# A three-part network on one core: modulation columns taken in pairs, h and k made between the weight blocks, one weight tile in four multiplied as float32

## The reference

```python
silu_c = jax.nn.silu(c)
silu_cc = jax.nn.silu(c_ctx)
shift, scale, gate = jnp.split(silu_c @ w_ada[l] + b_ada[l], 3, axis=-1)
shift_c, scale_c, gate_c = jnp.split(silu_cc @ w_ada[l] + b_ada[l], 3, axis=-1)
h = _modulate(_rmsnorm(xs, norm_g[l]), shift[:, None], scale[:, None])
hc = _modulate(_rmsnorm(cs, norm_g[l]), shift_c, scale_c)
pc_kv = hc @ w_l[:, OFF_K:OFF_ZA]
p = h @ w_l
```

## Time and profile before

| | before |
|---|---|
| median of 3 runs | 2229.89 us (2226.3 to 2232.34) |
| the profiled execution | 2231.75 us, its span 2230.1 us |
| PE busy | 2096.8 us, 94% of the span |
| DVE, ACT busy | 1357.2 us (61%), 1120.2 us (50%) |
| weight tiles split on ACT and DVE | 338, two units each |
| granted TensorE clock, mean | 0.973 of full |

### The profile page before, as it was taken

How to read it: one execution, slowest core, us unless ns; L and a number is a source line. 1 busy time by engine, 2 the same in 40 slices (tenths; PEclk the granted TensorE clock), 3 DMA queues, 4 the chain that set the end, 5 groups by cost and what they waited for, 6 DMA issues and landing times.

```text
span 2230.1 us, 32794 instructions
## 1 busy us (share of the span) xinstructions
PE 2096.8 (94%) x13142; PEld 1879.5 (84%) x13142; DVE 1357.2 (61%) x1766; ACT 1120.2 (50%) x1502; POOL 49.2 (2%) x60
## 2 busy tenths in 40 slices
PE   4879999999999997999999999999899999999996
PEld 3668888879999887899998788888689999998785
DVE  4864665556665555466676566766754643776554
ACT  5842445544443345244446666666544443775433
POOL 0000000000000000000000000010000000000000
PEclk9989999999999998999999899999999999999998
DMA  9942542347885554345555455555544455434552
GB/s 352 338 170 95 170 168 98 117 131 275 272 281 170 189 189 142 123 161 188 171 189 176 146 188 187 188 171 206 176 140 153 149 184 162 123 116 165 194 189 76
DMA packets 204236, 394.66 MB, mean 177 GB/s; under 512 B 6726, under 2 KB 25916, under 8 KB 201692
## 3 DMA queue, kind: packets, MB, share of 16 engines
q1 hardware_dynamic: 199584, 369.78, 49.7%
q0 software_dynamic: 2880, 17.40, 2.0%
q10 hardware_dynamic: 1660, 5.90, 0.7%
HBM read 390.89 MB, written 2.16 MB: 176 GB/s over the span
## 4 chain that ended last, share of the span: by engine, by line
PE 85%; DVE 6%; ACT 4%; issue 2%; DMA 2%; ACTq 0%; DVEq 0%; POOL 0%; SPq 0%
PE ps L1841 13%; PE ps L1843 13%; PE ps L1842 13%; PE ps L1829 12%; PE ps L1831 12%; PE ps L1830 12%; ACT w_hi L449 2%; DVE w_lo L1037 2%; DMA tables<-in_tables 1%; PE ps L2023 1%; PE ps L2001 1%; DVE tables L1352 1%; PE ps L2192 1%; PE ps L2193 1%; PE ps L2191 1%
## 5 line engine op out<-in xcount | busy, mean ns | idle before, releaser
L1037 DVE TENSOR_TENSOR w_lo<-raw,w_hi 128x1024 fp32r<-128x1024 f32 (+1 forms) x676 | 814.9, 1221 | 681.0 <-ACT w_hi L449 680.3
L449 ACT ACTIVATE w_hi<-raw 128x1024 fp32r<-128x1024 f32 (+1 forms) x676 | 701.2, 1052 | 752.8 <-PE ps L1843 371.8
L1841 PE MATMUL ps<-act,w_hi 128*128 128x256 f32 x2048 | 587.8, 287 | 7.6 <-DVE w_lo L1037 6.2
L1842 PE MATMUL ps<-act,w_hi 128*128 128x256 f32 x2048 | 580.8, 284 | 0.0
L1843 PE MATMUL ps<-act,w_lo 128*128 128x256 f32 x2048 | 580.7, 284 | 0.0
L1841 PEld LDWEIGHTS ps<-act,w_hi 128*128 128x128 f32 x2048 | 394.2, 192 | 12.2 <-DVE w_lo L1037 7.3
L1842 PEld LDWEIGHTS ps<-act,w_hi 128*128 128x128 f32 x2048 | 394.5, 193 | 2.3 <-issue 2.2
L1843 PEld LDWEIGHTS ps<-act,w_lo 128*128 128x128 f32 x2048 | 394.3, 193 | 0.0
L1829 PE MATMUL ps<-w_hi,act 128*128 128x512 f32 (+1 forms) x640 | 252.3, 394 | 8.3 <-issue 7.4
L1831 PE MATMUL ps<-w_hi,act 128*128 128x512 f32 (+1 forms) x640 | 248.0, 387 | 0.0
L1830 PE MATMUL ps<-w_lo,act 128*128 128x512 f32 (+1 forms) x640 | 247.7, 387 | 0.0
(11 more groups left out here) (282 smaller groups left out, 2445.5 us busy)
## 6 DMA issues: line engine op xcount, KB each, us to landing
raw<-in_ssd_w_in SPq DMA_DIRECT2D x80, 1024.0 KB, 5.2
raw<-in_w_in SPq DMA_DIRECT2D x72, 1024.0 KB, 5.2
raw<-in_w_ada SPq DMA_DIRECT2D x48, 1024.0 KB, 5.6
raw<-in_dsa_w_in SPq DMA_DIRECT2D x36, 1024.0 KB, 5.0
raw<-in_ssd_w_out SPq DMA_DIRECT2D x32, 1024.0 KB, 5.1
raw<-in_dsa_w_out SPq DMA_DIRECT2D x32, 1024.0 KB, 5.1
raw<-in_w_out SPq DMA_DIRECT2D x16, 1024.0 KB, 5.1
raw<-in_w_proj_a SPq DMA_DIRECT2D x12, 1024.0 KB, 5.2
```

The lines of the kernel that those rows point to most:

```text
L449: e.activation(w_hi[:, nth(u) % SPLIT, :, :w], raw[:, t % RAW, 2 * h:2 * h + 2, :w], ACT.Copy).then_inc(hi_done, 1)
L1037: e.tensor_tensor(w_lo[:, slot, :, :w], raw[:, t % RAW, 2 * h:2 * h + 2, :w], w_hi[:, slot, :, :w].bitcast(F32), ALU.subtract).then_inc(lo ...
L1841: e.matmul(o, wh, hi, start=first and f % 2 == 0, stop=False, skip_group_check=True)
L1842: e.matmul(o, wh, lo, start=False, stop=False, skip_group_check=True)
```

## The change

- The blocks of w_ada come in pairs of shift and scale for the same 512 features (`ADA_ORDER`: 0, 4, 1, 5, 2, 6, 3, 7), so that a quarter of the features is ready after two blocks. `modulate(q)` does bias and gain for that quarter.
- The four tiles of the key block become a segment "key", one after each of blocks 4 and 5 of the new order and two after the last (`ADA_KEYS`). h is made quarter by quarter and `keys(j)` multiplies key tile j when quarter j of h is there. Values follow as block 1.
- The last tile of each modulation block (`unsplit`) isn't split. `modulation_rest` multiplies its four chunks, as they were loaded, as float32 with the high and low columns of c (`bitcast(F32)`), and `unsplit_used` counts it. SP waits for that count instead of `lo_done` before it loads over such a tile; `lows` counts the units that DVE has split. ACT and DVE leave these 16 units out.
- PE's modulation is no loop any more, and the streams of ACT, DVE and PE up to the value block are written out anew. The rows live in two halves of a buffer (`ROWS`) and the modulation alternates between PSUM banks 4 and 5; the turned rows go to bank 7, the turned x to banks 0 to 3.

The diff, cut (PE's order in full, ACT's and DVE's where they wait for h):

```diff
+ADA_ORDER = (0, 4, 1, 5, 2, 6, 3, 7)
+ADA_KEYS = ((), (), (), (), (0,), (1,), (), (2, 3))
...
-    blocks("ada", 8, 4)
-    blocks("in", 10, 4)
+    for b, after in zip(ADA_ORDER, ADA_KEYS):
+        for j in range(4):
+            tiles.append(("ada", b, j, 1, CB))
+        for j in after:
+            tiles.append(("key", 0, j, 1, CB))
+    for b in range(1, 10):
+        for j in range(4):
+            tiles.append(("in", b, j, 1, CB))
...
+def unsplit(tile):
+
+    return tile[0] == "ada" and tile[2] == 3
...
             def load(n, b, i=0, step=0):
                 seg, _, j, _, w = TILES[n]
-                if n >= RAW or not isinstance(i, int):
-                    sp.wait_ge(lo_done, 2 * (n - RAW) + 2 + 2 * step * i)
+                if n >= RAW and unsplit(TILES[n - RAW]):
+                    sp.wait_ge(unsplit_used, sum(unsplit(t) for t in TILES[:n - RAW + 1]))
+                elif n >= RAW or not isinstance(i, int):
+                    sp.wait_ge(lo_done, lows(2 * (n - RAW) + 2) + 2 * step * i)
...
@@ ACT @@
+            splits(4, 2)
+            square(0)
+            splits(6, 4)
+            square(1)
+            splits(10, 2)
+            square(2)
+            splits(12, 2)
+            square(3)
+            splits(14, 4)
+            root(sm[:, 40:44], sm[:, 36:40], S["mean1"], 1, S["root1"])
...
+            splits(28, 2)
+            h_copy(0)
+            for n in range(3):
+                splits(32 + n, 1)
+                h_copy(1 + n)
+            splits(35, 2)
+            h_copy(4)
+            splits(37, 1)
+            h_copy(5)
+            splits(40, 1)
+            h_copy(6)
+            splits(41, 1)
+            h_copy(7)
+            splits(42, 1)
+            h_high(0)
+            splits(43, 1)
+            h_high(1)
+            splits(44, 3)
+            h_high(2)
+            splits(47, 1)
+            h_high(3)
+            splits(48, 13)
+            h_high(4)
+            splits(61, 1)
+            h_high(5)
+            splits(62, 10)
+            h_high(6)
+            h_high(7)
+            splits(72, 2)
...
@@ DVE @@
             def affine(n):
                 v, q = n % 2, n // 2
+                e.wait_ge(S["mod_ready"], q + 1)
+                e.wait_ge(S["h_copied"], 8)
...
+            splits(36, 5)
+            modulate(1)
+            splits(41, 1)
+            affine(0)
+            affine(1)
+            splits(42, 2)
+            h_low(0)
+            h_low(1)
+            ada_rows(4)
+            splits(44, 2)
+            affine(2)
+            affine(3)
+            splits(46, 2)
+            h_low(2)
+            h_low(3)
+            splits(48, 6)
+            ada_rows(5)
+            splits(54, 4)
+            modulate(2)
+            affine(4)
+            affine(5)
+            splits(58, 4)
+            h_low(4)
+            h_low(5)
+            splits(62, 2)
+            ada_rows(6)
+            splits(64, 8)
+            ada_rows(7)
+            modulate(3)
+            affine(6)
+            affine(7)
+            h_low(6)
+            h_low(7)
...
@@ PE @@
+            def modulation_rest(p):
+
+                t = ADA[p] + 3
+                e.wait_ge(raw_landed[t % RAW], landed(t))
+                for c in range(4):
+                    ins = e.matmul(ps[:, 4 + p % 2, :], cols[:, 12 + c, :].bitcast(F32), raw[:, t % RAW, c, :],
+                                   start=False, stop=c == 3)
+                ins.then_inc(unsplit_used, 1)
...
+            modulation(3, 0, 2)
+            turn_rows(2)
+            turn_xn(0)
+            for n in range(3):
+                modulation(3, 2 + n, 1)
+                turn_xn(1 + n)
+            modulation(3, 5, 1)
+            modulation_rest(3)
+            e.wait_ge(dve_freed, 3)
+            modulation(4, 0, 1)
+            turn_xn(4)
+            modulation(4, 1, 1)
+            turn_rows(3)
+            turn_xn(5)
+            for n in range(2):
+                modulation(4, 2 + n, 1)
+                turn_xn(6 + n)
+            modulation(4, 4, 2)
+            modulation_rest(4)
+            keys(0)
+            e.wait_ge(dve_freed, 4)
+            modulation(5, 0, 2)
+            turn_rows(4)
+            modulation(5, 2, 4)
+            modulation_rest(5)
+            keys(1)
+            e.wait_ge(dve_freed, 5)
+            modulation(6, 0, 2)
+            turn_rows(5)
+            modulation(6, 2, 4)
+            modulation_rest(6)
+            e.wait_ge(dve_freed, 6)
+            modulation(7, 0, 2)
+            turn_rows(6)
+            modulation(7, 2, 4)
+            modulation_rest(7)
+            keys(2, lambda: turn_rows(7))
+            keys(3)
```

More of the change, by code:

```diff
@@ L169, in build, with lows @@
         FIRST.setdefault(t[0], n)
-    SPLITS = [0]
+    SPLITS, LOWS = [0], [0]
     for t in TILES:
-        SPLITS += [SPLITS[-1] + (not by_vector(t))] * 1
-        SPLITS += [SPLITS[-1] + (not by_vector(t))] * 1
+        for _ in range(2):
+            SPLITS.append(SPLITS[-1] + (not by_vector(t) and not unsplit(t)))
+            LOWS.append(LOWS[-1] + (not unsplit(t)))
     def nth(u):
         return SPLITS[u]
+    def lows(u):
+        return LOWS[u]
     def landed(tile):
@@ L199, in build @@
                 BLOCKS.extend([(seg, "dve")] * 4)
-        elif seg not in ("head_q", "head_kv") and all(seg != s for s, _ in BLOCKS):
+        elif seg not in ("head_q", "head_kv", "key") and all(seg != s for s, _ in BLOCKS):
             nb = 1 + max(t[1] for t in TILES if t[0] == seg)
@@ L232, in ready @@
     def ready(seg, b=0):
-        per = 2 * sum(t[:2] == (seg, 0) and not by_vector(t) for t in TILES)
-        return nth(2 * FIRST[seg]) + per + per * b
+        b0 = TILES[FIRST[seg]][1]
+        per = 2 * sum(t[:2] == (seg, b0) and not by_vector(t) for t in TILES)
+        return nth(2 * FIRST[seg]) + per + per * (b - b0)
     with ExitStack() as ctx:
@@ L295, in tile_source @@
             k0 = j * 512
+            if seg == "key":
+                return [(0, 4, rows(a["w_in"], k0, COL_K))]
             if seg == "ada":
@@ L1130, in affine, with h_low @@
                                     ALU.mult, ALU.add).then_inc(S["h_affine"], 1)
[L1131 to L1134, removed]
+            def h_low(n):
                 e.wait_ge(S["h_hi"], n + 1)
@@ new lines, in turn_xn, with keys, body @@
+            def turn_xn(n):
+                src = gatedf if n < 4 else side
+                e.wait_ge(S["xn_ready"], 2 if n < 4 else 4)
+                e.wait_ge(S["rows_in"], 16 * 5)
+                if n >= 2:
+                    e.wait_ge(S["h_copied"], n - 1)
+                turn4(lambda c, tt: src[:, tt * D + c * P:tt * D + (c + 1) * P], n % 4,
+                      2 * (n % 2)).then_inc(S["h_turned"], 1)
+            def keys(j, between=None):
+                e.wait_ge(S["h_lo"], 2 * j + 2)
+                for m in range(2):
+                    def body(c, slot, m=m):
+                        kc = 4 * j + 2 * m + c
+                        ins = tokens_out([0, 1, 2, 3],
+                                         [tok(act, kc, 0), tok(act, kc, 1), tok(gated, kc, 0), tok(gated, kc, 1)],
+                                         kc, slot, c, kc == 0, kc == 15)
+                        if between and m == 0 and c == 0:
+                            between()
+                        return ins
+                    unit(2 * KEY[j] + m, 0, 0, body)
@@ new lines, in _ @@
+            e.wait_ge(S["c_ready"], 1)
+            ADA = [n for n, t in enumerate(TILES) if t[0] == "ada" and t[2] == 0]
+            KEY = [n for n, t in enumerate(TILES) if t[0] == "key"]
+            assert BI["ada"] == 0 and ADA[4] == 16 and KEY[0] == 20
+            modulation(0, 0, 6)
+            modulation_rest(0)
+            modulation(1, 0, 2)
+            turn_rows(0)
+            modulation(1, 2, 4)
+            modulation_rest(1)
+            e.wait_ge(dve_freed, 1)
+            modulation(2, 0, 2)
```

179 lines of the change are left out of this document (86 added, 93 removed).

## The result

The changed kernel takes 2230.85 us (median of 20 runs, 2228.79 to 2239.17), the one before 2226.99 us (20 runs, 2222.88 to 2234.44): ratio 1.0017, 95% interval 1.0009 to 1.0025. It is **slower by 3.9 us**; no change (-0.15 us) was forecast, with 2229.7 us. That is less than the 0.3% that the prediction called measurable; 20 runs resolve it. That 2229.7 lies so near to 2230.85 is luck: it was counted down from the three runs shown then (2229.89), and the same kernel's 20 runs have a median 2.9 us lower.

A forecast was written before the change was run, and what follows sets the result against it. PE, busy 94% of the span, was the bound, so only its waits could give time. First keys at 98.4 plus 79.7 us gave 178.1, plus 4 for two clock drops 182.1: effect -0.15 us, 2229.7 us, range 2219 to 2238.

The forecast's parts named there:

- T: Start of the value block, where the change ends; forecast 182.1 us against 182.25 before, so an effect of -0.15 us.
- float32 call: One float32 matmul of 512 columns on PE: two records, 0.86 us; four per unsplit tile, 3.44 us.
- first key unit (K): PE's start on the first key tile, between the modulation blocks; forecast at 98.4 us after a wait of 6.3 us.
- keys(0) with its drop: First key tile on PE: 10.9 us at full clock, with a 2.0 us clock drop charged for the wait before it.
- block 7 with its drop: Last modulation block: 13.4 us including a 3.6 us wait for a row copy, with a 2.0 us clock drop charged.
- the walk from block 0 to the first keys: Step-by-step timing of blocks 0 to 4, each time the latest of its inputs; ended with keys starting at 98.4 us.
- The loads behind PE's products: Loads queued until PE's float32 product frees a buffer: 3.0 us behind another; uncertainty in T -1.5 to +3 us.
- the length of a drop: Work lost when PE's clock falls to half after a wait: 2.0 us each, charged twice, 4 us.
- Rival (a): Tiles 8, 16 and 20 land before ACT wants them; keys start at 93.0, effect -9.6 us, 2220.3 us; chance 0.27.
- Rival (b): PE falls to half clock at waits of blocks 3, 5 and 6, 2.6 us each; +7.6 us, 2237.5 us; chance 0.10.
- Rival (c): Float32 call costs more than two records; at four, 3.44 us a tile more, about 2237 us; chance 0.03.
- The rule weighed: Short compute between waits returns PE to half rate; applied to all waits of the walk, where the forecast charged two.

The follow-up runs named there:

- e5: Changed kernel with the fourth tile of block 3 (tile 15) split instead of multiplied as float32; one run, 2232.6 us.
- e9: Changed kernel with the turning of rows 1 moved behind all six units of block 2; one run, 2229.6 us.
- e3: Changed kernel with the turning of row pair 6 four units later in block 7; 2.9 us above the kernel before.
- e10: Changed kernel with h made earlier, fourth tiles of blocks 3 and 6 split, row copy 7 ahead of splits 70 and 71; 3.9 us below the kernel before.
- e8: Changed kernel with h of quarters 1 and 2 made earlier and the fourth tile of block 3 split; 1.9 us below the kernel before.
- e1: Changed kernel with every modulation tile split, so no float32 product; 12.8 us above the kernel before.
- e6: Changed kernel with h of quarters 1 and 2 made earlier, ahead of splits, same work; 0.8 us above the kernel before.
- e11: Kernel before, in its old order, with the float32 product in blocks 0 to 2 only; 3.9 us above the kernel before.
- e2: Kernel before, in its old order, with one modulation tile in four multiplied as float32 in all blocks; 4.3 us above the kernel before.

## Why the prediction went wrong

**The order of events held, the sum did not.** The forecast was T = 182.1; it is 187.0. By its steps:

| step | forecast | measured | |
|---|---|---|---|
| float32 call | 0.86 us | 8 records, 0.43 us apart | right |
| product of block 0 ends | 39.3 | 40.2 (its last record 39.73 + 0.43) | +0.9 |
| ACT takes tile 8 | 47.4 | 48.34 | +0.9 |
| product of block 2 ends | 63.0 | 65.9 (62.42 + 3.44) | +2.9 |
| ACT takes tile 16 | 71.4 | 74.05 | +2.7 |
| product of block 3 ends | 78.7 | 81.4 (78.00 + 3.44) | +2.7 |
| ACT takes tile 20 | 86.8 | 90.78 | +4.0 |
| first key unit (K) | 98.4, wait 6.3 | 102.13, wait 6.93 | +3.7 |
| keys(0) with its drop | 12.9 | 12.4 | -0.5 |
| block 5, keys(1), block 6 | 32.6 | 32.9 | +0.3 |
| block 7 with its drop | 15.4 | 16.6 | +1.2 |
| keys(2), keys(3) | 22.8 | 23.0 | +0.2 |

*The step that failed is the walk from block 0 to the first keys*, which brought 3.7 of the 4.9 us. The table parts them. In block 2 it lost 2.0 us: there the walk follows ACT alone and leaves out PE's wait of 3.05 us for the row copy and the drop behind it, 3.4 us at half clock or 1.7 us of work. The loads behind PE's products are the term it gave -1.5 to +3 us. From the end of a product until ACT takes the tile behind it, it has 8.1, 8.4 and 8.1 us for tiles 8, 16 and 20, and 8.2, 8.2 and 9.3 were measured: right for two, 1.2 us short for the third, which landed 8.7 us after its issue at 82.04, where tiles 8 and 16 took 7.5 and 7.6. The start was 0.9 us late by the end of block 0's product, and the chain from tile 20 to K 0.3 us shorter than forecast. e5 fits this: with tile 15 split K comes 4.4 us earlier, though not by the loads alone. e9 gives back 0.75 us of block 2; how much of its 2.0 would reach the keys stays open.

*The second term is the length of a drop.* I took 2.0 us; the one in block 7 cost 3.5 (7 us at half), the one at the first keys 1.4 (102.13 to 104.85 at 0.43 us). In the sum of the two it is 4.9 against 4.0. e3 shows that it is the clock: 0.79 there and 1.00 without the wait.

*Rival (a), loads not late,* had T - K = 79.7 and K = 93.0. e5 has tile 20 in time and K = 97.7, and e10 reaches T - K = 79.0 by other edits. Its guess that a wait of 3.6 us leaves the clock alone came true in e8 (3.50 us) and not in e5 and e10 (3.38 and 3.51 us). *Rival (b), a drop at each wait,* has no case at its own places: behind the 1.80 us of block 3 and the 1.30 us of block 5 PE's pace stays 0.23 us, and block 6 has no wait. The drop that came unasked is in block 2. *Rival (c)* is out by the eight records.

*The rule weighed.* The Trainium skill, "TensorE: Matmul & The Clock Gate", section "HAM oscillation — how this bites in real kernels", has the engine fall back after each wait of its example, in which some 2 us of matmuls stand between waits of 3 to 5 us. The prediction stretched this to all waits of the walk. The traces agree in part: the waits of 3.05, 3.23 and 6.93 us had a drop behind them, those of 2.58, 1.80 and 1.30 us had none. But the length of the wait alone doesn't decide it, in either reading: 2.22 us in e1 (pace 0.43 us from 130.96 on) and 2.43 us in e6 had a drop, 3.50 us in e8 had none.

*What the prediction didn't ask* is what bounds the kernel before between 40 and 122 us. It read ACT at 39.97 of 40 us, with the DMA at 0.98 beside it. e11 shows the loads to be the bound there: ACT's relief gave nothing, and a buffer held longer cost 2.7 to 3.6 us even where PE had room.

What stays open: why tile 20 took 8.7 us to land and tile 16 7.6 us; why T moves by up to 2.6 us more than the median. T of one execution carries the drops that this execution happened to have, as e8 and e10 below show; whether that is the reason isn't shown.

## What to carry to other kernels

When work moves from the engines that free a buffer to a later engine in the chain, price the loads behind that buffer first: here SP issues the loads in order, so one late release delayed all loads behind it, at a DMA share of only 0.87 and 0.59. Removing work from an engine that is full gave nothing here, where the DMA was full beside it; take the work away alone, as e2 and e11 do, before counting on it. Two parts that each lose more alone (13.4 and 6.9 us) can lose less together (4.8), and the rest came from the order on DVE: make what PE waits for before the splits that wait for PE.

## What the runs showed of the hardware

The same wait leaves drops of different length. In the changed kernel the wait of 3.23 us before the turning of rows 6 was followed by 7 us at half clock, in e9 a wait of 3.24 us at the same place by half as much: its block 7 has a clock of 0.90 over 16.4 us, 3.3 us at half, and the turning took 1.15 us in place of 1.69.

```profile
145.80:162.20 16.40, 13.16 (x45) 8.64 (x44) 13.67 (x13) 8.79 (x9) 0.00 (x0) 0.90 0.79 285
```
```profile
152.44 1.15 PE L2044 MATMUL ps<-tables,actf 4*128 4x2 f32 x8 [3.24 <-DVE actf L1171]
```

At the first keys it is the same with equal waits. e8 waits 3.50 us and goes on at full clock. e10 waits 3.51 us and runs at half clock until 102.6, 5.5 us, though both have the same code up to there:

```profile
97.84 0.50 PE L1948 MATMUL ps<-w_hi,act 128*128 128x512 f32 x1 [3.50 <-DVE gated L1157]
98.18 0.39 PE L1949 MATMUL ps<-w_lo,act 128*128 128x512 f32 x1
```
```profile
97.68 0.63 PE L1950 MATMUL ps<-w_lo,act 128*128 128x512 f32 x1
...
102.37 0.56 PE L1949 MATMUL ps<-w_hi,act 128*128 128x512 f32 x1
```

So of the waits measured here some were followed by a drop of 1.4 to 3.5 us of work, half of the time at half clock, and others of the same length by none; it is not a constant of 2.0. This also bears on the experiments: T - K of e8 (80.5) has no drop at the first keys in it and that of e10 (79.0) has 2.8 us, so the edits of e10 may be worth more than the 1.5 us between them.
